# Attention of a two-layer hybrid decoder: value products in pairs, row maxima in a three-row block, a new head and tail of the attention stage, and the mask of the row-ordered scores added by VectorE

## What is computed

```python
def _causal_attention(q, k, v):          # 8 heads, q and k of 96 columns, v of 64
    scale = 1.0 / float(np.sqrt(q.shape[-1]))
    for s, e in bounds:
        sc = einsum('bqhd,bkhd->bhqk', q[:, s:e], k[:, :e]) * scale
        causal = arange(e)[None, :] <= arange(s, e)[:, None]
        probs = softmax(where(causal, sc, -inf))
        outs.append(einsum('bhqk,bkhd->bqhd', probs, v[:, :e]))
```

## Time and profile before

| what | value |
|---|---|
| three runs | 3776.69, 3779.09 and 3779.88 us, median 3779.09 |
| the profiled execution | 3780.01 us, its span 3778.2 us |
| TensorE busy in the span (matmul) | 3607.8 us, 95% |
| VectorE, ScalarE, GpSimd | 2379.1 (63%), 1303.6 (35%), 1416.5 (37%) |
| mean granted TensorE clock | 0.985 of full |
| matmuls | 29127 |

### The profile page before, as it was taken

The page is one execution under the profiler, slowest core; times in us unless marked ns, Lnnn a source line. Parts: engine busy times, 40 slices in busy tenths (PEclk is TensorE's granted clock), DMA queues, the critical chain, the costliest instruction groups (busy, mean ns, idle before and its releaser), DMA issues. The chain is left out here.

```text
span 3778.2 us, 69294 instructions
## 1 busy us (share of the span) xinstructions
PE 3607.8 (95%) x29127; PEld 3285.7 (87%) x29127; DVE 2379.1 (63%) x2811; ACT 1303.6 (35%) x1894; POOL 1416.5 (37%) x789
## 2 busy tenths in 40 slices
PE   6989999999999999999999999999999999999998
PEld 6666989988798999989985679888879989999997
DVE  2255446756468877776833653485655698777677
ACT  5244124312213444453432521351231144444434
POOL 4054850000252655544412559200003536555341
PEclk9999999999999999999999999999999999999999
DMA  4421666522431222263234228554224222222732
GB/s 118 127 54 48 216 203 191 172 74 55 137 93 70 83 74 80 84 247 121 89 74 128 58 76 263 180 178 138 69 82 131 61 80 80 85 80 74 260 124 83
DMA packets 475705, 438.10 MB, mean 116 GB/s; under 512 B 105808, under 2 KB 400940, under 8 KB 475420
## 3 DMA queue, kind: packets, MB, share of 16 engines
q1 hardware_dynamic: 455164, 382.22, 33.8%
q10 hardware_dynamic: 20255, 51.78, 3.7%
HBM read 296.88 MB, written 137.05 MB: 115 GB/s over the span
## 5 line engine op out<-in xcount | busy, mean ns | idle before, releaser
L278 POOL TENSOR_TENSOR w_hi<-w_raw,consts 128x1024 fp32r<-128x1024 f32 (+1 forms) x78 | 140.7, 1804 | 1203.3 <-DMA w_raw<-in_w_proj_rwkv 831.2
L232 PE MATMUL psum<-h_hi,w_hi 128*128 128x348 f32 x1632 | 355.9, 327 | 15.3 <-SPq L1353 8.5
L232 PE MATMUL psum<-h_lo,w_hi 128*128 128x348 f32 x1632 | 350.3, 323 | 0.0
L232 PE MATMUL psum<-h_hi,w_lo 128*128 128x348 f32 x1632 | 348.9, 322 | 0.0
L232 PEld LDWEIGHTS psum<-h_hi,w_hi 128*128 128x128 f32 x1632 | 277.2, 190 | 22.1 <-SPq L1353 9.5
L232 PEld LDWEIGHTS psum<-h_lo,w_hi 128*128 128x128 f32 x1632 | 278.7, 190 | 0.0
L232 PEld LDWEIGHTS psum<-h_hi,w_lo 128*128 128x128 f32 x1632 | 276.3, 189 | 0.0
L3084 POOL TENSOR_TENSOR piece_lo_w<-sum,piece_hi_w 128x512 fp32r<-128x512 f32 x120 | 209.5, 1746 | 133.9 <-ACT piece_hi_w L3397 131.0
L3129 PE MATMUL psum<-t_lo,piece_hi_w 128*128 128x260 f32 x1280 | 258.1, 283 | 0.0
L3129 PE MATMUL psum<-t_hi,piece_hi_w 128*128 128x260 f32 x1280 | 257.8, 283 | 0.0
L3129 PE MATMUL psum<-t_hi,piece_lo_w 128*128 128x260 f32 x1280 | 257.1, 282 | 0.0
(11 more groups left out here) (589 smaller groups left out, 9517.6 us busy)
## 6 DMA issues: line engine op xcount, KB each, us to landing
w_raw<-in_w_in SPq DMA_DIRECT2D x68, 512.0 KB, 10.5
wsum<-in_w_down SPq DMA_DIRECT2D x88, 256.0 KB
wsum_scratch<-wsum SPq DMA_DIRECT2D x22, 1024.0 KB
raw_g<-in_w_up SPq DMA_DIRECT2D x40, 512.0 KB, 3.8
raw_v<-in_w_up SPq DMA_DIRECT2D x40, 512.0 KB, 3.9
gate_scratch<-gst ACTq DMA_DIRECT2D x32, 522.0 KB, 3.0
gbuf<-gate_scratch SPq DMA_DIRECT2D x32, 522.0 KB, 3.7
prep_scratch<-prep ACTq DMA_DIRECT2D x8, 2080.0 KB, 8.3
```

Source lines behind the costliest of these rows:

```text
L232: last = nc.tensor.matmul(bank[:, n, :], w(k), x(k)[:, nrange(n)], start=(k == 0 and q == 0), stop=(k == kt - 1 and q == 2))
L278: nc.gpsimd.tensor_tensor(w_hi[s][:, 0:width], w_raw[s][:, 0:width], consts[:, 4:5].broadcast_to([P, width]), ALU.mult).then_inc(hi_done.s ...
```

## The change

- **Value products in pairs.** `outputs` runs in every second step, for two steps at once; `pt` has four buffers instead of three (`NPT`). Row sums move from steps 5, 11 and 2 to steps 6, 12 and 1.
- **Maxima in three rows.** `nm` becomes a block of 35 columns (both heads' maxima in columns 0 and 32, the rest zero), so that one matmul turns both heads' maxima; three rows of q_hi and of ones in k_hi take part in the first product (`NSH`). There are two such blocks, in turn.
- **Mask by VectorE.** The mask product of `rows_of_scores` goes; `maximum` first adds `mask_row` to the last 128 columns in PSUM (a new VectorE instruction), waits for it, and then takes the maximum.
- **Order.** For pairs 1 to 3 the rows of group 2 lie in steps 1 to 5 (2, 1, 2, 1, 2 of them) and not one in each of steps 0 to 7; the shifts move from steps 2, 8, 16 to 1, 7, 15.
- **Head.** The rows and maxima of blocks 0 to 2, and all four low parts of pair 0, move into the end of the latent phase (three of the low parts on GpSimd, one on VectorE); the rounding of pair 0 moves ahead of the last value copies. The attention phase starts with `shift_rows`.
- **Splits.** The two units for the next phase are split in quarters, one quarter in each of steps 10 to 13 of pairs 0 and 1.
- **Tail.** Tile 0 of the RWKV projection phase is done at the end of the attention phase, with the last row sums inside it.
- **Buffers.** The sums go into `yst` itself, two of them in turn, and ScalarE's copy waits for the store of the last but one.

The diff's core (the mask product goes, the two orders change, the tail and the head are new):

```diff
             if s < 8:
-                own = rows_in(2)
-                first, more = (s, 1) if g else ((2 * (s - 3), 2) if s < 6 else (s, 1))
+                first, more = ((2 * (s - 3), 2) if s < 6 else (s, 1)) if g == 0 else ((s // 2) + s - 1, 1 + s % 2) if 0 < s < 6 else (0, 0)
...
-            return [(g, 0)] if s == 5 else [(g, 1)] if s == 11 else [(g - 1, 2)] if s == 2 and g else []
+            return [(g, 0)] if s == 6 else [(g, 1)] if s == 12 else [(g - 1, 2)] if s == 1 and g else []
+
+        def outputs_at(n):
+
+            return [n - 2, n - 1] if n >= 2 and n % 2 == 0 else []
+
+        def quarter_at(n):
+
+            g, s = divmod(n, PS)
+            return (g, s - 10) if g < 2 and 10 <= s < 14 else None
...
-                    if hi == b * BLK + rows:
-                        last = mm(row_view(m, hi - lo - rows, hi - lo, rows), ident_r[0:rows, 0:rows], mask_row[0:rows, 0:rows], start=False, stop=True, skip_group_check=True)
...
-                        last = mm(psum[0:1, ring_bank(x), at:at + rows], nm[e][0:rows, b:b + 1], ident_r[0:rows, 0:rows], start=True, stop=True)
+                    last = mm(psum[0:32 + NSH, ring_bank(x), at:at + rows], nm[(NG * g + G) % 2][0:rows, b - blocks_in(G)[0], :], ident_r[0:rows, 0:rows], start=True, stop=True)
...
-                for r in rows_in(0):
-                    rows_of_scores(0, *r)
-                keep_warm(7, 2)
                 shift_rows(0, 0)
...
+                outputs(NS - 2)
                 outputs(NS - 1)
-                keep_warm(0, 2)
-                row_sums(*last_group)
+                pe.wait_ge(dves.sem, dves.of(0, row_taken(len(row_order) - 1)))
+                pe.wait_ge(next_lo, 8)
+
+                def between(k):
+                    if k == 2:
+                        row_sums(*last_group)
+                product(pset[0], KD, wtile(w_hi[0], KD), wtile(w_lo[0], KD), hk(h_hi), hk(h_lo), between).then_inc(next_tile, 1)
+                pe.wait_ge(next_tile, 1)
...
+                    if hi == b * BLK + rows:
+                        corner = row_view(m, hi - lo - rows, hi - lo, rows)
+                        dves.did(nc.vector.tensor_tensor(corner, corner, mask_row[0:rows, 0:rows].bitcast(F32), ALU.add), f"mask{g}_{b}_{e}")
+                        dve.wait_ge(dves.sem, dves.of(0, f"mask{g}_{b}_{e}"))
...
+                nc.gpsimd.memset(nm[0][:, :, :].bitcast(F32), 0.0).then_inc(early_done, 1)
+                for e in range(2):
+                    for x, (raw, hi) in enumerate(((k_raw0[e], k_hi0[e]), (q_raw0[e], q_hi0[e]))):
+                        if e and x:
+                            continue
+                        pool.wait_ge(early_hi[e], 2)
+                        nc.gpsimd.tensor_tensor((k_lo0, q_lo0)[x][e][:, :], raw[:, :], hi[0:QK, :], ALU.subtract).then_inc(early_lo, 1)
...
-                tile(0, 0)
+                pe.sem_inc(used.sem, 1)
                 tile(1, 1)
```

More of the change, by code:

```diff
@@ L636, in layer @@
         mask_row, mask_col = masks_r[:, 0:BLK], masks_r[:, BLK:2 * BLK]
-        assert cursor[0] <= 229344
+        nm = [after("nm0", [P, NSH, 32 + NSH], F32R)]
+        assert cursor[0] <= 229376
+        q_lo0 = [place(f"q_lo0{e}", [QK, TP], F32R, pair_at + row_bytes * e) for e in range(2)]
+        k_lo0 = [place(f"k_lo0{e}", [QK, TP], F32R, pair_at + row_bytes * (2 + e)) for e in range(2)]
         cursor[0] = early_at
@@ L776, in _ @@
                 pe.wait_ge(u_acts.sem, u_acts.of(0, f"cp{copied[-1]}"))
-                keep_warm(0, 4)
+                pe.wait_ge(early_done, 6)
+                m = 0
+                for b in blocks_in(0):
+                    for e in range(2):
+                        pe.wait_ge(early_hi[e], 2)
+                        if m >= 2:
+                            pe.wait_ge(first_max, m - 1)
+                        n, block = (b + 1) * BLK, slice(b * BLK, (b + 1) * BLK)
+                        nc.tensor.matmul(psum[:, 2 * (m % 2), 0:n], q_hi0[e][0:QK, block], k_hi0[e][0:QK, 0:n], start=True, stop=True)
+                        nc.tensor.matmul(psum[:, 2 * (m % 2), b * BLK:n], ident_r[:, :], mask_row, start=False, stop=True, skip_group_check=True).then_inc(first_rows, 1)
+                        m += 1
+                keep_warm(7, 2)
             @block.scalar
@@ L878, in layer @@
         racc = [after(f"racc{p}", [P, 2, QW]) for p in range(2)]
-        nm = [after(f"nm{e}", [P, NKB], F32R) for e in range(2)]
+        nm.append(after("nm1", [P, NSH, 32 + NSH], F32R))
         nm_last = [after(f"nm_last{e}", [P, 2]) for e in range(2)]
@@ L949, in layer @@
             g = n // PS
-            rows = rows_at(n) if n >= 0 else [(0, *r) for r in rows_in(0)]
+            rows = rows_at(n) if n >= 0 else []
             shifts = shifts_at(n) if n >= 0 else [(0, 0)]
@@ L968, in layer @@
             if n < 0:
-                dve_n += [f"lo0_q{e}" for e in range(2)]
-                pool_n += [f"lo0_k{e}" for e in range(2)] + [f"one{e}" for e in range(2)]
+                pool_n += [f"zero{p}" for p in range(1, 2)] + [f"one{e}" for e in range(2)]
             else:
@@ L1056, in _ @@
                 store_group(RT - 1, 2)
[L1057 to L1058 removed]
+                sp.wait_ge(y_out[0], 16 * (RT * NG // 2))
             @block.gpsimd
```

187 lines of the change are left out of this document (104 added, 83 removed).

## The result

| | before | after |
|---|---|---|
| median of the runs (six each, in turn) | 3779.49 us | 3807.61 us |
| lowest and highest | 3776.69, 3788.36 | 3795.09, 3813.58 |
| the profiled execution, its span | 3780.01, 3778.2 | 3807.31, 3805.3 |
| mean granted TensorE clock | 0.985 | 0.972 |
| matmuls | 29127 | 28899 |

The ratio is 1.0072 (95% interval 1.0057 to 1.0087): the change makes the kernel 28 us slower. The forecast was 3767 us, with a range to 3785.

What follows compares the result with a forecast made beforehand. TensorE was taken to bound the kernel, with VectorE's chain behind the division as late and becoming the bound. Layer 0's -6.7 and layer 1's -5.5 us made -12.2 from 3780.0, 3767.8; median 0.9 lower, 3767 us; range 3747 to 3785.

Steps and rivals of the forecast that it cites:

- the price of the clock: TensorE's lower clock behind the wait in step 14: 1.3 us lost each time, bounds 0 and 3.
- The wait in step 14: TensorE stands some 3.5 us at the rows of block 3, until VectorE has done division and low part.
- The 1.4 us more a pair for that bound: VectorE's chain behind the division makes each pair followed by another 44.7 us against 43.33, three times a layer.
- The mask: VectorE's addition of the mask in PSUM: about 0.29 us, 0.33 with the wait, bounds 0.20 and 0.45.
- Pair 0's bubble: TensorE's wait for an exponential in pair 0 goes: -8.2 us in layer 0, -5.4 in layer 1, clock included.
- priced +0.6: Pair 0's shift of group 1 waits for two more masks: 0.6 us lost in each layer.
- The last pair: The pair without successor saves 1.5 us a layer: TensorE's 3.3 less 1.8 for its rows of steps 1 to 5.
- The head: Start of the attention phase: first scores at 185.4 instead of 187.82, -2.4 us in both layers, bounds -4.5 and +0.5.
- The tail: From attention's end through the next phase's tiles: -3.3 us in layer 0, -4.9 in layer 1, bounds -1 and -6.
- the third: Rival: VectorE's chain grows further through low parts waiting for GpSimd and masks of 0.45 us; slower, 3798 us; chance 0.13.
- The first rival: VectorE doesn't bind, no wait in step 14 lowers the clock, each pair saves 2 us: 3739 us; chance 0.25 including a middle course.

Runs made afterwards that it cites:

- lows_early: after, with VectorE's low parts q0 and k0 of the next pair done behind steps 9 and 10 instead of 12 and 14; 3808.21 us, ratio 1.0079.
- all_mended: lows_early with group 1's division in step 13, GpSimd's head low parts held until head 1 is rounded, pair 0's step 2 value products before the shift; 3788.51 us.
- all_mended_mask_back: all_mended with the row mask as TensorE's product again, not added by VectorE; 3750.74 us, ratio 0.9935.
- wait_put_in: all_mended_mask_back with the division back in step 12 and three extra unused maxima on VectorE ahead of block 2's; 3789.50 us, ratio 1.0035.
- mask_alone: before, with only the addition of the row mask moved from TensorE to VectorE; 3828.54 us, ratio 1.0118.
- warm: after, with 22 dummy TensorE products of 128 columns ahead of the rows of step 14 in pairs 0 to 2; 3799.25 us, ratio 1.0054.
- wait_small: wait_put_in with one extra maximum on VectorE instead of three; 3773.45 us, ratio 0.9987.
- mask_blocks_4_5: all_mended_mask_back with the head's low parts shared two and two by GpSimd and VectorE, and VectorE masking blocks 4 and 5 only; 3774.82 us, ratio 0.9996.

## Why the prediction was wrong

- **The failing step is the price of the clock**: "I take 1.3 us each time (bounds 0 and 3)". It was read off one window of 4 us behind one wait, and before's loops have no stretch at half clock over 6.8 us. After's four long stretches are 27.3, 27.3, 13.7 and 13.7 us; at 0.42 they cost 11.5 and 5.7 us each. With the waits inside pair 0 it is 44 us over both loops for the forecast's 8. After's six runs have a mean clock of 0.970 to 0.974, before's of about 0.985, so some 100 us more at half; 42 us less than 3807.6 is 3766 (an estimate). The forecast without its 8 us for the clock is 3759, so the rest of the sum is out by 7 us only. That is in part luck, since terms below are wrong in both directions.
- **The wait in step 14**: right in place and mechanism, 2.9 us for 3.5. But it was read as a loss that VectorE's chain hides, since "VectorE has become its bound". lows_early shortened that chain and gained nothing. The 1.4 us more a pair for that bound had the wrong sign: with 0.42 us taken off for each us at half clock, after's pairs 1 and 2 are 42.3 to 42.9 us long (an estimate), for 43.33 before.
- **The mask**: 0.29 us as forecast (0.28 in the row of 228.75). That it costs a few tenths each and no more was wrong: it costs 22 us in after and 38 in all_mended, most of it through the clock.
- **Pair 0's bubble**: gone as forecast, but a wait of 1.75 us for the last maximum at 194.5, priced +0.6, left 10.2 us at half clock in either layer; pair 0, with 13.6 us more at half behind step 14, is no shorter (55.45 for 54.56, and in layer 1 55.34 for 51.38).
- **The last pair**: forecast -1.5, measured +0.9 in layer 1 at a clock of 1.00 (36.88 for 35.97), and 35.89 in all_mended_mask_back, with the mask on TensorE. Two waits of after are missing there: 0.69 us for VectorE's last low part at the pair's start, and 0.47 us for a maximum, at the rows of its last block. I had taken 1.8 us for such losses, and a gain was left over.
- **The head**: -2.4 forecast, -0.2 in layer 0 (first scores at 187.57 for 187.82) and -0.6 in layer 1 (from the first value projection to the first scores 31.5 us for 32.2). VectorE's rounding was carried over at 0.69 us and not seen to lie beside GpSimd's low parts: 2.23 and 2.87. The Trainium skill's page "SBUF — State Buffer" (section "SBUF: two separate sides") has the port pair that both share as a lock held for a whole instruction. The rows agree: GpSimd's first two low parts end at 175.69 and 178.49, and VectorE's roundings, 0.69 us long when alone, end 0.55 us behind them, at 176.25 and 179.04. I had called it stretching and priced the lock for one low part only.
- **The tail**: -3.3 and -4.9 forecast, -7.5 and -4.7 measured; what I let count in layer 0 for GpSimd's weights (1.6) and its chain didn't show.
- **The rivals**: the third had the sign and a chance of 0.13, by another mechanism: one of three low parts waited for a GpSimd instruction (k_lo 3.15 us, q_lo 1.44 and 1.23), the mask took 0.29 and not 0.45, and what decided was the clock, which the rival priced at 1.7 us a transition; that it had the sign is luck. The first rival, that VectorE doesn't bind, is near the truth for the lists alone (0.4 to 1.0 us saved a pair by the estimate above, where it had 2), but its 3739 took the clock for granted.

## What to carry to other kernels

Price a new wait of TensorE by what the clock does behind it, not by its length: here the clock held behind before's 0.7 us, while 1 to 3 us of waiting could be followed by nothing or by up to 41 us at half speed, at about 0.42 us lost for each. The run-to-run scatter grows with it (the runs of the versions with under 30 us at half clock spread over 5 to 11 us, those of the others over 14 to 28, before's over 8 to 16). Work taken off TensorE is no gain if it lengthens the list of an engine that TensorE waits for; put it where that engine has pauses, or leave it. When work is moved next to another engine's, take its duration from a row with that neighbour, not from where it stood before.

## What the runs showed of the hardware

- The lower clock can last long without TensorE idling: 26.81 us busy of 27.31, 40.71 of 40.96, and 17.07 of 17.07. Identical waits of one kernel were followed by 13.7, 3.4 and 6.8 us of it (wait_put_in), in another by 41 us or none (mask_alone).
- In warm, with the wait filled, the clock fell at 247.11 and 291.49 though no wait of TensorE in the 8 us before was longer than 0.62 us.
- Runs of one kernel line up with their own clocks: all_mended's fastest (3771.85 us) had 0.981, one of 3793.7 us had 0.972, so 0.32 us for each us more at half clock. A line through the runs of wait_small gives 0.49, through those of mask_blocks_4_5 0.24.
- An addition of 128 columns into PSUM takes VectorE 0.29 us, a rounding of 96 x 1044 takes it 0.69 us alone and up to 2.87 beside a GpSimd subtraction.
